# The ring's four places join the places of gathered rows at row 592 instead of row 642

## The reference

```python
def expert_block(args):
    hx, ex, gx = args
    a = jnp.einsum('td,thkd->thk', hx, u_tab[ex]).astype(jnp.float32)
    w = (gx * jax.nn.gelu(a, approximate=False)).astype(hx.dtype)
    return jnp.einsum('thk,thkd->td', w, v_tab[ex])
```

## Time and profile before

| | us |
|---|---|
| median of 3 runs | 4147.08 |
| lowest, highest run | 4146.43, 4155.8 |
| the profiled execution | 4148.36 |
| its span, first to last instruction | 4146.3 |
| PE busy | 3362.4 (81%) |
| DVE busy | 2813.4 (68%) |
| POOL busy | 1448.8 (35%) |
| DMA, mean rate over the span | 342 GB/s |

### The profile page before, as it was taken

The page is one execution under the profiler, slowest core; times in us unless marked ns, Lnnn a source line. Parts: engine busy times, 40 slices in busy tenths (PEclk is TensorE's granted clock), DMA queues, the critical chain, the costliest instruction groups (busy, mean ns, idle before and its releaser), DMA issues.

```text
span 4146.3 us, 38906 instructions
## 1 busy us (share of the span) xinstructions
PE 3362.4 (81%) x14121; PEld 2505.5 (60%) x14121; DVE 2813.4 (68%) x3542; ACT 380.7 (9%) x954; POOL 1448.8 (35%) x1094
## 2 busy tenths in 40 slices
PE   7799889999999989979999999999999999100000
PEld 5466678888855555457777777777777777100000
DVE  5354442227678786786666889996775556769998
ACT  0311110000212111010000020000000000100000
POOL 0000000000014453444434244434333566777764
PEclk9999999999999999989999999999999999555555
DMA  8578555557459999999999989999999999889997
GB/s 332 212 261 304 211 201 203 204 217 296 165 212 381 389 366 387 415 398 379 408 406 409 421 342 377 391 393 417 415 398 378 418 403 395 315 309 410 410 395 320
DMA packets 253425, 1416.34 MB, mean 342 GB/s; under 512 B 35472, under 2 KB 84576, under 8 KB 88256
## 3 DMA queue, kind: packets, MB, share of 16 engines
q0 software_dynamic: 124704, 841.18, 50.5%
q1 hardware_dynamic: 68832, 501.25, 30.8%
q10 hardware_dynamic: 59744, 72.06, 5.0%
HBM read 1363.27 MB, written 51.10 MB: 341 GB/s over the span
## 4 chain that ended last, share of the span: by engine, by line
PE 56%; DMA 13%; DVE 12%; POOL 10%; issue 6%; DVEq 1%; ACT 1%; ACTq 0%; PEld 0%; PEldq 0%; POOLq 0%; SPq 0%
PE pq L436 56%; DMA first<-peer_u,experts 6%; DVE pq L1746 6%; POOL got L1922 5%; POOL first L1904 5%; DMA first<-peer_v,experts 4%; DMA ring<-wstream 2%; DVE first L1736 2%; DVE ring L1259 1%; POOL ring L1904 1%; DVE late L1257 1%; ACT arena L816 0%; PE pq L440 0%; DVE late L1746 0%; DMA ring<-peer_v,experts 0%
## 5 line engine op out<-in xcount | busy, mean ns | idle before, releaser
L436 PE MATMUL pq<-h_last,ring 128*128 128x288 f32 (+2 forms) x6688 | 1640.0, 407 | 7.3 <-ACT h_last L816 5.0
L436 PEld LDWEIGHTS pq<-h_last,ring 128*128 128x128 f32 (+2 forms) x6688 | 1253.5, 188 | 383.6 <-issue 16.3
L1904 POOL DMA_INDIRECT first<-peer_u,experts x256 | 405.8, 1585 | 1710.0 <-DVEq L1581 1205.9
L1904 POOL DMA_INDIRECT first<-peer_v,experts x464 | 634.7, 1368 | 810.8 <-DVEq L1747 723.8
L436 PE MATMUL pq<-first,ring 128*128 128x256 f32 (+2 forms) x3104 | 690.0, 384 | 19.1 <-DMA ring<-wstream 12.7
L1736 DVE CUSTOM_DVE_ANT_0 first<-first,late 128x2048 f32<-128x2048 f32 x256 | 582.2, 2292 | 179.6 <-DMA first<-peer_u,experts 170.7
L1746 DVE SCALAR_TENSOR_TENSOR late<-first,wts,late 128x2048 f32<-128x2048 f32 x254 | 597.2, 2351 | 153.3 <-DMA first<-peer_v,experts 138.6
L436 PEld LDWEIGHTS pq<-first,ring 128*128 128x128 f32 (+2 forms) x3104 | 580.0, 188 | 123.1 <-DMA ring<-wstream 14.7
L1746 DVE SCALAR_TENSOR_TENSOR pq<-first,wts,pq 128x2048 f32<-128x2048 f32 x142 | 334.5, 2355 | 94.8 <-DMA first<-peer_v,experts 86.0
L1922 POOL DMA_INDIRECT got<-dots_dram,at_dot x288 | 327.4, 1137 | 106.3 <-issue 106.3
L436 PE MATMUL pq<-arena,cst 128*32 128x512 f32 x8 | 5.5, 847 | 417.2 <-ACTq L1232 417.2
(11 more groups left out here) (201 smaller groups left out, 1980.2 us busy)
## 6 DMA issues: line engine op xcount, KB each, us to landing
ring<-wstream SPq DMA_DIRECT2D x478, 1024.0 KB, 7.8
dots_dram<-wts ACTq DMA_DIRECT2D x8, 2304.0 KB, 8.7
dots_dram<-stage ACTq DMA_DIRECT2D x128, 144.0 KB, 9.0
first<-peer_v,experts POOLq DMA_INDIRECT x464, 11.4
got<-dots_dram,at_dot POOLq DMA_INDIRECT x288, 8.1
first<-peer_u,experts POOLq DMA_INDIRECT x256, 10.1
out<-arena ACTq DMA_DIRECT2D x6, 512.0 KB, 7.8
o_last<-x_t ACTq DMA_DIRECT2D x5, 576.0 KB, 15.1
```

What stands on the lines that cost most here:

```text
L436: return nc.tensor.matmul(out, lhsT, rhs, start=start, stop=stop)
L1904: g.indirect_dma_start(out=slots[slot], out_offset=None, in_=peer_u if kind == "u" else peer_v, in_offset=bass.IndirectOffsetOnAxis(ap=exp ...
```

## The change

`N_WIDE`, the entry from which on eight places are handed round, was `TAIL + 2 * FB * R_ALT` = 642 and becomes `TAIL + 78` = 592. Entries 592 to 595 are in the places of `first` either way. Entries 596 to 641 so far went round the four places of `first`; now they go round eight, and the first gather into `ring` is that of entry 596 (batch 10, row 2) instead of 646 (batch 16, row 4). The wait for `a_ps` moves with it. Nothing else is touched: the same rows are gathered in the same order, and the instructions are the same in kind and number.

```diff
@@ -377,7 +377,7 @@
         N_GATES, N_VAR0, N_SCALE0, N_LAST, N_NEED = 438, 458, 480, 502, TAIL - 1
         SORT_STEPS = 26
         uses = [0] * (GR + RING)
-        N_WIDE = TAIL + 2 * FB * R_ALT
+        N_WIDE = TAIL + 78
         ENTRY = []
         for n, (kind, t, c) in enumerate(ORDER):
             slot = n % GR if n < N_WIDE else (n - N_WIDE) % (GR + RING)
```

## The result

| | before | changed |
|---|---|---|
| median of 20 runs, us | 4149.12 | 4137.55 |
| lowest, highest | 4137.70, 4159.35 | 4129.41, 4144.19 |
| span of the profiled execution | 4146.3 | 4138.9 |

The ratio of changed to before is 0.9969, with a 95% interval of 0.9961 to 0.9977. So the change makes the kernel 0.31% faster, 10 to 16 us by the interval. That is just at the bound of 0.3% which the prediction took for telling it from no change. The predicted 4137.2 us compares with 4137.55. That the two agree to 0.4 us is in part luck: the prediction started from a median of three runs, 4147.08, and with 20 runs the kernel before has 4149.12, 2.0 us more. The forecast gain was 9.9 us and the medians differ by 11.6, so two misses of about 2 us cancel.

What follows compares the result with a forecast made beforehand. From 3536.5 to 3700.8 us POOL was held up by few places and by instructions lengthened by DVE's SBUF additions. Terms: -14.2 + 4.3 = -9.9 us, from a median of 4147.08 to 4137.2 us; 8-in-10 range 4130 to 4146.

Steps and rivals of the forecast that it cites:

- Part 1: Entries up to 595 keep their places, so nothing before the gather of entry 596 changes: 0.
- Part 2: Wait for PE, moved from entry 646 to 596, is already fulfilled there: 0, with 11.7 us to spare.
- Part 3: POOL's waits for a place between 3537 and 3709 us go: -14.2 us, allowing 3 us left.
- Part 4: Batches 11, 13, 15: one more POOL instruction each lengthened by DVE's SBUF additions: +4.3 us, bounds -0.8 to +16.0.
- Part 5: More rows in flight could make the row of entry 646 land later: taken as 0, bounds 0 and +6.0 us.
- Part 6: From entry 642 on, everything moves ahead as a whole by what POOL has gained by entry 646.
- The whole of the gap goes: Rival: six batches take batch 18's 20.5 us each, -41 us, 4106 us; gain over 14 us given 0.15.
- The blocking gets dearer: Rival: each blocked POOL instruction loses 1.92 us, net +1.8, 4148.9 us; 0.13 together with no effect.
- The wait for PE decides: Rival: PE ends over 11.7 us later, POOL stands at entry 596; slower, 4160 us; chance 0.06.

Runs made afterwards that it cites:

- e1: Changed kernel with the sum of tile 3 moved from SBUF to PSUM at batch 11 instead of batch 28; ratio to before 0.9865.
- e2: Kernel before (four places up to entry 641) with the sum of tile 3 in PSUM from batch 11 on; ratio to before 0.9941.
- e7: Changed kernel with the sum of tile 2 also kept in SBUF in batches 10, 12 and 14; ratio to before 1.0053.
- e9: The changed kernel itself, timed and profiled a second time; ratio to before 0.9967.
- e6: Changed kernel with the wait for PE and the first gather into ring at entry 592 instead of 596; ratio to before 0.9976.
- e5: Changed kernel with the wait for PE and the first gather into ring at entry 588 instead of 596; ratio to before 1.0009.
- e3: Changed kernel with only five places handed round from entry 592 to 641, eight from 642 on; ratio to before 0.9975.
- e4: Changed kernel with the wait for PE and the first gather into ring at entry 580 instead of 596; ratio to before 1.0065.

## Why the prediction was right, point by point

**What bounds the stretch.** Right: two things, places and lengthened instructions, and the change removes the first alone. Taking away the second (e1, e2) and doubling it (e7) moved the time as this says, and the table leaves nothing over for a third.

**Part 1, nothing before entry 596.** Right as far as can be seen. The start of entry 596 differs by 3.1 us from one profile to the other, but in the other direction in e9 (3535.76), so it is scatter between executions.

**Part 2, the wait for PE: 0.** Right. Entry 596 starts 0.30 us behind entry 595, while PE ended 12 us earlier. The margin is small: four entries sooner POOL stands for 2.10 us, eight entries sooner for 24.5 (e6, e5).

**Part 3, -14.2.** Right, and the 3 us that I allowed for waits on entry n-8 were not needed. Nor were all eight places: with five, 3.6 us of waits remain (e3), and in the trace of the changed kernel no entry is issued before the addition of entry n-6 has ended. The lead of four or five rows that the prediction gave POOL was the right measure.

**Part 4, +4.3.** The mechanism was right to the count, 24 in place of 21. The size was +3.0, not +4.3: the average fell from 1.43 us (30.1 / 21, which the prediction had as 1.44) to 1.38. The runs show a scatter of this, 32.7 to 34.9 us for 24 in the six profiles with that count, which is +2.6 to +4.8 against before. So the term lies in it, and the bounds of -0.8 and +16.0 were far wider than the scatter.

**Part 5, 0 (up to +6).** Missed by a little. Entry 646 is used 8.6 us behind its issue, not 5.8, and its addition waits 2.10 us for the row. Rows do land later here: from 3550 to 3690 us the median is 7.3 us for places of `first` and 9.5 for those of `ring`, where it was 7.3 before, with `first` alone. Most of that is recovered by batch 18: from there to the end both kernels take 398.9 us, and from the issue of entry 646 to batch 18 it is 39.1 us in place of 38.2. So +0.9 in this profile. Over the six profiles of kernels with 24 lengthened instructions the time from entry 646 to the end is 436.7 to 438.5, against 437.0 before, so I would not call this a term of its own.

**Part 6, a mere shift.** Right, by those same numbers.

**The sum.** -14.2 + 3.0 + 0.9 = -10.3, and the profiles differ by 10.5 from entry 596 on; forecast -9.9. The timing gives 0.9969, 12.9 us, with 9.9 us (0.9976) at the edge of the interval. The forecast took the gain for within 0.3%, and it has come out at 0.31 by the ratio and 0.28 by the medians. On which side of the bound it lies isn't told by this measurement, so the forecast of "just inside" is neither borne out nor refuted. The terms were right by themselves, but for part 4's 1.3 us too much and part 5's 0.9 us too little, which cancel in part.

**The rivals.** "The whole of the gap goes" failed for the reason given, and e1 shows that it takes the other half of the work: with eight places and the sum in PSUM the six batches take 129.1 us in place of 164.3, with the rival's 20.5 us a batch (20.5 to 20.7) in five of them. "The blocking gets dearer" by holding each other up in turn: the average of a blocked instruction went down, not up to 1.92 us. The additions in the rows above follow one another at 2.47 us while an instruction of POOL overlaps the start of each, so DVE isn't held up. The Trainium skill ("SBUF — State Buffer", section "Who interferes with whom") says that a VectorE instruction with two inputs in SBUF contends with a GpSimd instruction that reads SBUF, and one with at most one SBUF input, outside VectorE's 2-port modes, does not. The gathers here take their indices from SBUF, and the trace agrees: 0 of 102 instructions are lengthened in e1, and one for each of the 48 additions in e7. The rule of the Trainium skill ("SBUF — State Buffer", section "SBUF: two separate sides") that whichever of the two starts first has the ports for its whole instruction agrees only for POOL behind DVE. "The wait for PE decides" did not happen, and it is cheaper than priced: the prediction had a us of loss per us of waiting, and e4 and e5 show 40 us for 54.8 and 17 for 24.5, some 0.7. While PE is at work POOL waits for places as well. Entries 587 and 588 in POOL's timeline, changed kernel:

```profile
3502.98 0.94 POOL L1904 DMA_INDIRECT first<-peer_v,experts  x1 [2.26 <-DVEq L1747]
3507.27 0.94 POOL L1904 DMA_INDIRECT first<-peer_v,experts  x1 [3.35 <-DVEq L1747]
```

The wait for PE takes their place. From entry 579 to 596 the waits for places come to 13.2 us in the changed kernel, to 5.3 in e5 and to none in e4, less 0.30 us each. So the 54.5 us of e4 cost 54.5 - 13.2 = 41.3 (measured: 106.9 us from entry 579 to 596 in place of 65.0, 41.9 more), and the 24.2 us of e5 cost 24.2 - 7.9 = 16.3 (measured: 16.3).

## What to carry to other kernels

Before many buffers are added, count how far ahead the issuing engine really gets. A trace in which the buffers bind can't tell it: with four places no entry is issued before entry n-4 is released. The trace of the changed kernel can. Entry n is issued before the addition of entry n-5 has ended in four cases and before that of n-6 in none, so six places would do; in e1, where POOL is quick, it happens with n-6 in ten cases and with n-7 in none, so seven would. Neither number of places was run. An engine that waits for buffers and is also slowed by its neighbour hides a part of one cost behind the other; removing the wait brings the wait less what comes out from behind it (14.2 less 3.0 here), and removing both brings more than the two alone. When gathers are issued by GpSimd, look at where VectorE keeps its running sum: in this stretch, with eight places, moving it from SBUF to PSUM brought 33 us where the buffers had brought 11. Even with four places it brought 22.8 (171.7 to 148.9).

## What was not expected of the hardware

In all profiles of this stretch, each lengthened instruction of POOL ends 0.81 to 0.83 us behind the end of the addition that blocks it, often while the next addition already runs. One reading, argued and not tested, is that the first 0.1 of its 0.94 us is spent ahead of the block and the rest behind it. The cost of one block is then set by when POOL comes: it goes from 0.95 us above 0.94 (an instruction of 1.89 us in e6 and e9) to 2.1 us (one of 3.06 in e3). DVE's own additions into SBUF stay at 2.35 to 2.40 us throughout, as they do into PSUM (2.35 to 2.36).
